# A state-space layer whose scaled input moves from VectorE to GpSimd for six of eight channel tiles

## What is computed

```
h = rmsnorm(x)                                   # x * rsqrt(mean(x*x) + eps) * gain
u = h as 64 groups of 16 channels
bu = einsum('btgc,gpc->btgp', u, b_bar)          # 64 complex states a group
s  = associative_scan(lam_bar, bu)               # over time
y  = einsum('btgp,gcp->btgc', s, c).real + d*u
z  = gelu(y)
a, gate = split(z @ w_glu)
out = a * sigmoid(gate)
```

## Time and profile before

| what | value |
|---|---|
| median of 3 runs | 2186.64 us (2186.15 to 2188.95) |
| the profiled execution: its own time | 2188.33 us |
| the profiled execution: its span, first to last instruction | 2186.6 us |
| mean granted TensorE clock | 0.995 of full speed |
| the state-space loop in the profile | about 1620 to 1690 us |

### The profile page before, as it was taken

How to read it: one execution, slowest core, us unless ns; L and a number is a source line. 1 busy time by engine, 2 the same in 40 slices (tenths; PEclk the granted TensorE clock), 3 DMA queues, 4 the chain that set the end, 5 groups by cost and what they waited for, 6 DMA issues and landing times.

```text
span 2186.6 us, 42987 instructions
## 1 busy us (share of the span) xinstructions
PE 2142.7 (98%) x17360; PEld 2108.6 (96%) x17360; DVE 1600.6 (73%) x2462; ACT 906.9 (41%) x1284; POOL 5.7 (0%) x19
## 2 busy tenths in 40 slices
PE   9999999999999989999999999999989999999998
PEld 8999999999999889999999999999988999999998
DVE  5766776457878789778487887848797579686774
ACT  5222232234545455445155543515533345253443
POOL 0000000000000000000000000000000000000000
PEclk9999999999999999999999999999999999999999
DMA  5233543243242144445245242424374434242332
GB/s 142 77 90 105 161 128 108 73 116 80 60 117 60 52 117 113 129 125 146 63 128 138 68 124 85 142 64 116 109 218 149 108 91 124 84 137 87 97 88 81
DMA packets 439814, 234.91 MB, mean 107 GB/s; under 512 B 34849, under 2 KB 432370, under 8 KB 439666
## 3 DMA queue, kind: packets, MB, share of 16 engines
q1 hardware_dynamic: 426562, 218.76, 35.5%
q10 hardware_dynamic: 12528, 13.08, 1.8%
q0 software_dynamic: 576, 1.05, 0.3%
HBM read 212.67 MB, written 23.30 MB: 108 GB/s over the span
## 4 chain that ended last, share of the span: by engine, by line
PE 93%; DVE 5%; issue 1%; DMA 1%; ACT 1%; SPq 0%; DVEq 0%; ACTq 0%
PE ps L2519 52%; PE ps L2631 33%; PE ps L2748 2%; PE ps L2482 1%; PE ps L2938 1%; PE ps L2927 1%; PE ps L2913 0%; PE ps L2826 0%; DVE w_lo L1500 0%; DVE o_rs L2243 0%; DMA w_raw<-in_ffn_w_in_dram 0%; DMA wb<-wb_d 0%; PE ps L2790 0%; PE ps L2799 0%; PE ps L2817 0%
## 5 line engine op out<-in xcount | busy, mean ns | idle before, releaser
L2631 PE MATMUL ps<-hf_hi,s_hi 128*128 128x288 f32 x1848 | 547.6, 296 | 9.6 <-issue 4.5
L2631 PE MATMUL ps<-hf_lo,s_hi 128*128 128x288 f32 x1848 | 543.2, 294 | 0.0
L2631 PE MATMUL ps<-hf_hi,s_lo 128*128 128x288 f32 x1848 | 542.5, 294 | 0.0
L2631 PEld LDWEIGHTS ps<-hf_hi,s_hi 128*128 128x128 f32 x1848 | 346.9, 188 | 12.6 <-issue 7.2
L2631 PEld LDWEIGHTS ps<-hf_lo,s_hi 128*128 128x128 f32 x1848 | 347.2, 188 | 0.2
L2631 PEld LDWEIGHTS ps<-hf_hi,s_lo 128*128 128x128 f32 x1848 | 346.9, 188 | 0.0
L1588 DVE TENSOR_TENSOR s_lo<-s_raw,s_hi 128x1024 fp32r<-128x1024 f32 (+1 forms) x264 | 286.5, 1089 | 60.6 <-ACT s_hi L987 52.9
L987 ACT ACTIVATE s_hi<-s_raw 128x1024 fp32r<-128x1024 f32 (+1 forms) x264 | 250.2, 950 | 191.5 <-PE ps L2631 183.2
L929 ACT ACTIVATE w_hi<-w_raw 128x1024 fp32r<-128x1024 f32 (+4 forms) x141 | 185.7, 1323 | 242.4 <-PE ps L2519 239.4
L2519 PE MATMUL ps<-h_hi,w_hi 128*128 128x288 f32 x1216 | 267.8, 302 | 2.2 <-issue 1.1
L2519 PE MATMUL ps<-h_hi,w_lo 128*128 128x288 f32 x1216 | 260.5, 296 | 0.0
(11 more groups left out here) (415 smaller groups left out, 3081.1 us busy)
## 6 DMA issues: line engine op xcount, KB each, us to landing
s_raw<-in_ffn_w_in_dram SPq DMA_DIRECT2D x330, 256.0 KB, 3.3
w_raw<-in_ffn_w_out_dram SPq DMA_DIRECT2D x96, 256.0 KB, 3.2
w_raw<-in_ffn_w_in_dram SPq DMA_DIRECT2D x44, 512.0 KB, 5.1
w_raw<-in_hgrn_w_in_dram SPq DMA_DIRECT2D x32, 512.0 KB, 5.4
w_raw<-in_ffn_w_out_dram SPq DMA_DIRECT2D x48, 192.0 KB, 2.6
w_raw<-in_s_w_glu_dram SPq DMA_DIRECT2D x16, 512.0 KB, 5.1
w_raw<-in_ffn_w_out_dram SPq DMA_DIRECT2D x16, 384.0 KB, 4.0
w_raw<-in_ffn_w_out_dram SPq DMA_DIRECT2D x16, 320.0 KB, 3.7
```

The costliest lines, as they stand in the source:

```text
L2631: ins = M.matmul(out, w, h, start=f in (0, 1, 3) and k == 0 and n == 0, stop=f in (3, 5, 6) and k == KP - 1 and n == 2, skip_group_check=True)
```

## The change

scale_lifted for the tiles 2 to 7 is taken out of VectorE's states and written at the end of GpSimd's program as six instructions of the same size, each with the same wait for its tile's loads. In front of them GpSimd waits until VectorE has scaled tiles 0 and 1 (u_done at 2).

```
@@ gpsimd, behind the four adding transfers @@
+            def scale_lifted(ct):
+
+                pool.wait_ge(u_ld[ct], 16 * LIFT)
+                u = u_lift[:, G_CT * ct:G_CT * (ct + 1), :]
+                nc.gpsimd.tensor_tensor(u, u, rs8[:].unsqueeze(1).to_broadcast([P, G_CT, BLOCKS]), ALU.mult)\
+                    .then_inc(u_done, 1)
+
+            pool.wait_ge(u_done, 2)
+            for ct in range(2, NK):
+                scale_lifted(ct)
@@ vector, at the end of states(ct) @@
-                    if ct + 2 < NK:
-                        scale_lifted(ct + 2)
```

## The result

The changed kernel takes 2193.99 us (median of 8 runs, 2191.75 to 2196.40), the kernel before in the same comparison 2187.97 (8 runs, 2186.15 to 2188.95). The ratio is 1.0029 with a 95% interval of 1.0020 to 1.0038, so it is slower by 6.3 us (4.4 to 8.3); the medians differ by 6.0. The profiled execution of after has a span of 2192.2 us, 5.6 more than before.

A forecast was written before the change was run, and what follows sets the result against it. TensorE was taken to set the pace after 1633.8 us, with the end of states(0) on the path. VectorE hold-ups 5.1, wb(3) -1.1 and clock +1.2 gave +5.2 us: 2191.8 us, range 2186.0 to 2195.5.

The forecast's parts named there:

- The removal at 0: Six scalings leaving VectorE behind states(0), 4.0 us in all, lie where TensorE sets the path; costed at 0.
- The rival in which VectorE bounds the layer: VectorE is the real bound behind states(0) and its 4.0 us come back: 2182.6 us; chance 0.02.
- whatever VectorE has to do in between: In the state-space layer VectorE's round is tied to TensorE's through ScalarE; z_lo of tile 0 waits 1.37 us for z_hi.
- Turns with VectorE: In the sampled decay and states(0), GpSimd instructions hold VectorE up whole, five times: 5.1 us on states(0)'s end; chance 0.60.
- The signs: From_states(0) at about 1635, wb(3) leaving after 1638, low clock about 1634 to 1638, VectorE rows of 1 us and more.
- No interference: GpSimd reads SBUF beside VectorE at no cost, states(0) ends as before: 2186.6 us, within 0.5; chance 0.25.
- turns by element: VectorE is slowed only while GpSimd streams, some tenths an instruction: +0 to +1.5 us; chance 0.10.
- The 1.1 us: Length of one two-input GpSimd multiplication of 128x576, estimated from affine_select rows, with ends 0.64 and 1.54 us.
- The clock: TensorE idles 6.7 us before from_states(0), drops to 1.2 GHz, and from_states(0) takes 3.2 us: +1.2 us.
- Given back: Transfer wb(3), leaving later and alone, takes 5.9 us where it took 7.0: -1.1 us.
- The tie: SP sends wb(3) only after from_states(0), so the end of states(0) reaches block_adds(3) through wb(3).
- "As before" behind block_adds(3): From block_adds(3) on TensorE's work is as before, so none of the loss comes back there.

The follow-up runs named there:

- E1: The kernel before with the scaling of tiles 2 to 7 left out on both engines: 2187.75 us, ratio 0.9989 to the kernel before.
- E8: The kernel before with wb transfers sent earlier on SP's queue, wb(2) ahead of the last tile's loads: 2185.86 us, ratio 0.9985 to the kernel before.
- E9: E2 with the wb transfers sent earlier on SP's queue: 2185.11 us, ratio 0.9985 to the kernel before.
- E3: The kernel before, VectorE keeping its scalings, plus six GpSimd multiplications of the same shape that nobody reads: 2194.84 us, ratio 1.0024 to the kernel before.
- E4: The changed kernel with GpSimd's six multiplications replaced by memsets, which read nothing: 2188.39 us, ratio 0.9994 to the kernel before.
- E6: The changed kernel with GpSimd multiplying by a constant, so one input instead of two: 2189.09 us, ratio 1.0003 to the kernel before.
- E2: The changed kernel, but GpSimd scales tile ct only once states(ct-2) has ended: 2188.40 us, ratio 0.9991 to the kernel before.
- E10: The changed kernel with wb transfers sent earlier on SP's queue, wb(2) ahead of the last tile's loads: 2192.58 us, ratio 1.0017 to the kernel before.
- E7b: The changed kernel with 30 unused matmuls on TensorE ahead of from_states(0) to fill its wait: 2191.53 us, ratio 1.0015 to the kernel before.
- E5: The changed kernel with GpSimd's six multiplications covering half the columns, 288 of 576: 2192.47 us, ratio 1.0013 to the kernel before.

## Why the prediction was right, and where its sizes were off

The forecast was +5.2 us; the measurement is +6.3 by the ratio and +6.0 by the medians (the stage +6.23). Of the distance from 2191.8 to 2193.99, 0.8 us is this difference, and the rest is the median of before, which was 1.3 us higher in the comparison than in the three runs that the forecast started from.

**The removal at 0: right.** From block_adds(3) to the product the time didn't shrink; it grew from 51.27 to 51.83. E1, without the scaling on either engine, takes 51.15 there. The rival in which VectorE bounds the layer is out for this kernel. That VectorE is tied to TensorE "whatever VectorE has to do in between" was too strong: with wb sent early (E8) its scaling stands on the chain, and the removal would be worth some 0.5 us, by an estimate from one profile each of E8 and E9.

**Turns with VectorE: right, and shown** by E3 (the addition alone brings them) and E4 (not without reads). Five hold-ups and one under the three PSUM instructions, as forecast; 5.28 us on the end of states(0) against 5.1. The signs are there too: from_states(0) at 1634.90 (about 1635 was said), wb(3) leaving at 1639.48 (after 1638), the low clock from 1632 to 1639 (1634 to 1638). No interference is out, and turns by element, at some tenths an instruction, is out for this instruction. The Trainium skill states this rule under SBUF — State Buffer, "Who interferes with whom": a VectorE instruction with two inputs from SBUF contends with a GpSimd instruction that reads SBUF, and not with one that only writes. After, E3 and E4 agree (1.08 to 1.22 us, and none beside the memset). That one is fully blocked until the other ends, as the prediction has it from there, holds in after but for the last 0.15 us; in E6 VectorE goes on 1.14 us before GpSimd's one-input instruction ends.

**The 1.1 us: right in the sum, wrong in its meaning.** I took it as the length of GpSimd's instruction and the hold-up as the whole of that. The instruction takes 1.41 us alone (E2); the hold-up is 1.08 to 1.21, less than the whole. The two errors cancel, so the hit on this term was luck. The way to the 1.1, from the affine_select rows, also falls: E6 takes 1.84 us where that line gave 0.64. The Trainium skill's GPSIMD Engine Reference, "Elementwise — side-by-side cycle accounting", gave an estimate of 1.25 us for the two inputs, nearer to the 1.41 that E2 shows.

**The clock: the term was mis-sized.** +1.2 was forecast, +1.72 came: from_states(0) ran at 1.2 GHz throughout, 3.69 us, where I had scaled by the 81 and 50 ns of the block_adds, 1.6. That scale holds for block_adds (E10: 2.61 at the lower level for 1.56, 1.67), but not for from_states, whose own is 3.69 / 1.97 = 1.87. E7b sets the whole effect at 1.6 us at block_adds(3).

**Given back: right in kind, -1.5 for -1.1.** wb(3) took 5.5 us where it took 7.0. That it was alone this time fits, but no run tried it apart. The sum at block_adds(3) is 5.28 from VectorE, 0.18 from longer sums for the norm (3.69 for 3.51), 1.72 from the clock and -1.5, that is 5.68; measured 5.67.

**The tie: only one of two.** I named wb(3) as the carrier. It is a carrier: it lands within 0.1 us of the start of block_adds(3). But TensorE's own order, from_states(0) to the end of from_states(1), reaches 1644.68, only 0.34 us sooner, and E10 takes wb(3) out and leaves the delay where it was (partly by chance, as said there). Of TensorE's part the idle 1.96 us of before was used up, for wb(2) had long landed when from_states(0) ended. I had said that this work runs inside wb(3)'s time, which is so by 0.34 us, and hadn't said that it is as long.

**"As before" behind block_adds(3): nearly.** 0.56 us more came there, by block_adds(6), which waits 1.49 us in after's chain; in before it waits 0.7 for wb. The transfer of wb(6) sets this wait: from issue to landing it took 6.6 us in before, 7.2 in after, 7.4 in E2 (a wait of 1.66) and 5.8 in E7b (next to none), and in E10 the early wb removes it. So TensorE isn't "almost alone" behind block_adds(2), as the prediction read its chain, and the 0.56 us are the scatter of one transfer, which a forecast from one profile couldn't have. Why its time varies is not shown.

## What to carry over

Before work goes from VectorE to GpSimd, find the stretch in which it will run and read what VectorE does there: six instructions that VectorE held for 4.0 us off the path cost 5.3 us on the path, because they ran beside instructions with two SBUF inputs. Where the move is wanted, tie each instruction to a place at which VectorE reads PSUM or waits (E2: one line, and the loss is gone). And look at the wait that the profile gives to nobody: the 1.96 us of "issue" ahead of block_adds(2) were a transfer behind others on its queue, worth more to this kernel than what the change took off VectorE.

## What the hardware did that I had not expected

- The hold-up of VectorE isn't the length of GpSimd's instruction. Two inputs of 576 columns: 1.08 to 1.22 us of 1.41; two of 288: 0.47 to 0.60; one input of 576: 0.28 to 0.47 of 1.84; a memset of 0.58: none. The longer instruction holds less because it lets VectorE go 1.14 us before its end, the other two 0.13 to 0.16. What it does in that time is not shown; that it has half the reads fits.
- On GpSimd the multiplication by a constant took longer than the one by a tensor: 1844 ns against 1674 in the mean, both beside VectorE.
- Whether a wait lowers TensorE's clock doesn't follow from its length alone: from_states(0) ran at the full 1.97 us after waits of 1.59 (before) and 2.80 (E6), and slower after 2.49 (E9, 2.54 us), 2.58 (E2, 2.77 us) and 3.69 (E5, 2.98 us). What else decides was not tried.
